# A fused two-block model kernel on one core: router logits from x itself, row lookup in two parts, expert weights loaded slot by slot, biases in four row groups, expert places mixed

## The reference, cut to what matters

```python
x = x + g1[:, None, :] * mix                        # mix = concat(attention, ssm) @ w_out
h = _modulate(_rmsnorm(x, norm2_g[l]), sh2, sc2)    # h = norm(x) * norm2_g * (1 + sc2) + sh2
x = x + g2[:, None, :] * _moe(h, w_router[l], b_router[l], w1[l], b1[l], w2[l], b2[l])
...
logits = (hf @ w_router + b_router).astype(jnp.float32)     # 512 tokens x 32 experts
top_val, top_idx = lax.top_k(logits, TOP_K)                 # TOP_K = 4
gates = jax.nn.softmax(top_val, axis=-1)
...
gu = xb @ w1[e] + b1[e]; gate, up = jnp.split(gu, 2, axis=-1)
glu = gate * jax.nn.sigmoid(SWIGLU_ALPHA * gate)
((up + 1.0) * glu) @ w2[e] + b2[e]                          # per expert, on its own rows only
```

## Time and profile before

| what | value |
| --- | --- |
| median of 3 runs (lowest to highest) | 2327.5 us (2324.67 to 2331.74) |
| the profiled execution | 2333.3 us, span 2332.0 us |
| TensorE clock granted over the span | 0.949 of full speed |
| busy: PE, DVE, ACT, POOL | 91%, 26%, 15%, 2% |
| DMA | 554.64 MB, 238 GB/s over the span |

### The profile page before, as it was taken

The page is one execution under the profiler, slowest core; times in us unless marked ns, Lnnn a source line. Parts: engine busy times, 40 slices in busy tenths (PEclk is TensorE's granted clock), DMA queues, the critical chain, the costliest instruction groups (busy, mean ns, idle before and its releaser), DMA issues.

```text
span 2332.0 us, 35927 instructions
## 1 busy us (share of the span) xinstructions
PE 2121.3 (91%) x15835; PEld 919.6 (39%) x15835; DVE 595.4 (26%) x1120; ACT 353.0 (15%) x607; POOL 46.4 (2%) x54
## 2 busy tenths in 40 slices
PE   5999887699999999999999999736999999899997
PEld 2454444233433334433333333312444444444443
DVE  4983322311111101111110110154044343300002
ACT  2213412000000000000000000003143234200001
POOL 0000000000000000000000000010000000000000
PEclk7999987699999999999999999958999999999999
DMA  7355355696899999999999999660111111122211
GB/s 290 110 198 197 128 225 238 246 376 249 322 414 412 413 405 403 406 404 405 405 407 412 405 406 421 242 251 0 72 54 54 64 63 54 37 78 76 75 42 54
DMA packets 105787, 554.64 MB, mean 238 GB/s; under 512 B 11584, under 2 KB 22976, under 8 KB 56064
## 3 DMA queue, kind: packets, MB, share of 16 engines
q1 hardware_dynamic: 81984, 501.25, 54.1%
q10 hardware_dynamic: 18096, 31.55, 3.7%
q0 software_dynamic: 5552, 19.53, 2.5%
HBM read 525.94 MB, written 26.35 MB: 237 GB/s over the span
## 4 chain that ended last, share of the span: by engine, by line
PE 69%; SPq 12%; DMA 7%; DVE 5%; ACT 5%; issue 2%; ACTq 0%; DVEq 0%
PE psum L690 17%; SPq L325 11%; PE psum L864 10%; PE psum L815 10%; PE psum L698 8%; PE psum L431 6%; DMA arena<-in_w 4%; PE psum L684 3%; PE psum L807 2%; PE psum L873 2%; PE psum L407 1%; DMA ring<-in_mod_slabs 1%; DMA arena<-in_mod_slabs 1%; PE psum L706 1%; PE psum L851 1%
## 5 line engine op out<-in xcount | busy, mean ns | idle before, releaser
L690 PE MATMUL psum<-arena,ring 128*32 128x512 f32 x4288 | 479.9, 602 | 12.6 <-DMA arena<-in_w 12.6
L815 PE MATMUL psum<-h_t,ring 128*128 128x512 f32 x640 | 279.5, 594 | 0.7 <-ACT arena L1170 0.7
L690 PEld LDWEIGHTS psum<-arena,ring 128*32 128x32 f32 x4288 | 134.8, 111 | 357.1 <-issue 323.4
L698 PE MATMUL psum<-arena,h_t 128*32 128x256 f32 x3840 | 213.0, 380 | 9.8 <-DMA arena<-in_w 9.8
L1588 DVE TENSOR_SCALAR h_t<-psum 128x512 f32<-128x512 f32 (+2 forms) x33 | 27.9, 845 | 679.8 <-PE psum L690 679.8
L815 PEld LDWEIGHTS psum<-h_t,ring 128*128 128x128 f32 x640 | 120.6, 190 | 153.4 <-issue 151.9
L698 PEld LDWEIGHTS psum<-arena,h_t 128*32 128x32 f32 x3840 | 122.4, 110 | 92.8 <-DMA arena<-in_w 12.7
L1095 ACT ACTIVATE ring<-psum 128x512 f32<-128x512 f32 (+2 forms) x33 | 23.8, 720 | 740.5 <-PE psum L677 740.5
L690 PE MATMUL psum<-ring 128*32 128x512 f32 x1152 | 129.5, 600 | 5.1 <-DMA ring<-in_w 5.1
L431 PE MATMUL psum<-h_t,ring 128*128 128x512 f32 x256 | 115.0, 605 | 6.8 <-ACT h_t L919 6.8
L864 PE MATMUL psum<-h_t,ring 128*128 128x512 f32 x256 | 115.4, 605 | 4.7 <-DVE arena L1728 4.7
(11 more groups left out here) (390 smaller groups left out, 1738.5 us busy)
## 6 DMA issues: line engine op xcount, KB each, us to landing
arena<-in_w SPq DMA_DIRECT2D x288, 1024.0 KB, 28.1
ring<-in_w SPq DMA_DIRECT2D x96, 1024.0 KB, 29.4
ring<-in_mod_slabs SPq DMA_DIRECT2D x16, 2048.0 KB, 8.8
ring<-in_turn_slabs SPq DMA_DIRECT2D x40, 512.0 KB, 3.3
ring<-in_merge_slabs SPq DMA_DIRECT2D x32, 512.0 KB, 3.3
ring<-in_proj_slabs SPq DMA_DIRECT2D x24, 512.0 KB, 3.6
y_rows<-arena ACTq DMA_DIRECT2D x1, 10752.0 KB, 35.3
y_rows<-work ACTq DMA_DIRECT2D x72, 64.0 KB, 7.6
```

Of the source, the lines that this page charges most:

```text
L690: mm = pe.matmul(psum[32 * j:32 * j + 32, g, :], x_e[:, c * tokens + g * TG:c * tokens + g * TG + TG], slot[s][:, j * S:(j + 1) * S], star ...
L698: mm = pe.matmul(psum[32 * j:32 * j + 32, 6 + g // 2, (g % 2) * 256:(g % 2) * 256 + 256], h_e[:, g * 256 + half * P + 32 * c:g * 256 + hal ...
L815: mm = pe.matmul(psum[:, bank, :], ring[:, s, k, :], h_t[:, k, :], start=(k == 0), stop=(k == KT - 1))
```

## The change

Nothing is added to or taken from the result; the same values are computed by another route.

- The logits are taken from `x_t` itself. The router is scaled once by norm2_g*(1+sc2) (`gain`), and the share of sh2 in the logits is put into `brouter` by nine small matmuls ("router shift"). PE sums the products of four channel tiles each into four column groups (`logit_part`, parts 0 to 3 between slabs 22 and 23), DVE copies the four partial sums, and a matmul with the constant "stack" adds them and turns them to tokens. The root mean square of each token comes out as a column of 128 partitions x 4 (`square_sum`, on squares that DVE has added up on the way), and scales the logits (`row_scale`) and the stored rows. Shift and gain are applied later, in `keep_x`, by eight ACT instructions a pass instead of one.
- The waits of the routing are split (RANKS no longer waits for the "tokens ahead" matmuls), DVE's one-hots are single instructions, and the lookup is made in two parts: rows of the first four passes (`SOON`), then of the other 29. The gates are finished behind the lookup and turned on PE behind the first pass's up chunks.
- SP issues the clearing of `y_rows` and, behind it, 12 of the first 16 weight chunks before the last four slabs of w_out, each when its slot's buffer is free; the last four go out when the last slab has been used.
- b1 is loaded into four row groups of partitions, and the bias matmuls of group g read row group g.
- `PLACES` has another order.

```diff
-PLACES = [0, 1] + [2 + r for r in (15, 0, 16, 17, 1, 18, 2, 19, 3, 20, 4, 21, 5, 22, 6, 23, 7, 24, 8, 25, 9, 26, 10, 27, 11, 28, 12, 13, 14, 29)]
+PLACES = [0, 1, 17, 18, 19, 2, 20, 21, 3, 22, 23, 4, 24, 25, 5, 6, 7, 26, 8, 9, 27, 10, 11, 28, 12, 13, 29, 14, 15, 30, 16, 31]
...
+            sp.wait_ge(sem("arena zeroed"), 1)
+            sp.dma_start(y_rows[PLACE_ROWS:, :].rearrange("(b c) d -> c b d", c=ROWS),
+                         arena[:, 0:D].unsqueeze(1).to_broadcast([P, MAXO, D])).then_inc(sem("y cleared"), 16)
+
+
+            def load_chunk(n, s, e, c):
...
+            sp.wait_ge(sem("y cleared"), 16)
+            sp.wait_ge(sem("mod turned"), 9)
+            load_first(0, 1, 2, 3, 4, 5, 8, 9, 11)
+            sp.wait_ge(sem("head mixed"), 4)
+            load_first(6, 7, 10)
             for n in range(20, 24):
                 load_slab_of(n)
...
+            load_first(12, 13, 14, 15)
...
+            bank = pair_bank("router shift")
+            for k in range(KT):
+                pe.matmul(bank[:, 0:EXPERTS], mods[:, 24 + k:25 + k].to_broadcast([P, P]), router[:, k, :], start=(k == 0), stop=False, skip_group_check=True)
+            pe.matmul(bank[:, 0:EXPERTS], identity, brouter[:, :], start=False, stop=True, skip_group_check=True).then_inc(sem("router shifted"), 1)
...
+            def logit_part(k):
+                rows = slice(32 * (k % 4), 32 * (k % 4) + 32)
+                return pe.matmul(psum[rows, 4, :], router[:, k, :], x_t[:, k, :], start=(k < 4), stop=(k >= 4), skip_group_check=True)
+
+            def square_sum(k, first, last):
+                for t in range(TT):
+                    mm = pe.matmul(psum[:, 1, t:t + 1], h_t[:, k, t * P:(t + 1) * P], ones[:, 0:1], start=(first and t == 0), stop=last, skip_group_check=True)
+                return mm
...
+                if n == 22:
+                    pe.wait_ge(sem("router scaled"), 1)
+                    pe.wait_ge(sem("x mixed"), 4)
+                    for k in range(4):
+                        logit_part(k)
...
+            pe.wait_ge(sem("x mixed"), 7)
+            for k in range(4, 7):
+                logit_part(k)
+            pe.wait_ge(sem("squares added"), 6)
+            square_sum(0, True, False)
             pe.wait_ge(sem("x mixed"), 8)
-            rms_sum(1, h_t)
-            pe.wait_ge(sem("router loaded"), 16)
-            pe.wait_ge(sem("h ready"), 16)
+            logit_part(7).then_inc(sem("routing (PE)"), 1)
+            pe.wait_ge(sem("norm squares"), 16)
+            square_sum(7, False, True).then_inc(sem("norm sum"), 1)
+            pe.wait_ge(sem("routing (DVE)"), LOGIT_PARTS)
...
+                    mm = pe.matmul(psum[32 * g:32 * g + 32, 0, 0:SOON], hot_tok[:, n, :], hot_group[:, n, bass.ds(g, SOON, step=4)], start=(n == 0), stop=(n == TT * TOPK - 1), skip_group_check=True)
...
+                    mm = pe.matmul(psum[32 * g:32 * g + 32, 6, 0:NP - SOON], hot_tok[:, n, :], hot_group[:, n, bass.ds(4 * SOON + g, NP - SOON, step=4)], start=(n == 0), stop=(n == TT * TOPK - 1), skip_group_check=True)
...
-                        pe.matmul(psum[32 * j:32 * j + 32, g, :], which.to_broadcast([EXPERTS, TG]), b1_sb[:, j * S:(j + 1) * S], start=True, stop=False, skip_group_check=True)
+                        pe.matmul(psum[32 * j:32 * j + 32, g, :], which[EXPERTS * g:EXPERTS * g + EXPERTS, :].to_broadcast([EXPERTS, TG]), b1_sb[EXPERTS * g:EXPERTS * g + EXPERTS, j * S:(j + 1) * S], start=True, stop=False, skip_group_check=True)
...
-                act.activation(x_e[:, 0:KT * tokens].rearrange("p (b n) -> p b n", b=2), psum[:, 4:6, 0:4 * tokens], ACT.Copy).then_inc(sem("x_e kept"), 1)
+                for k in range(KT):
+                    act.activation(x_e[:, k * tokens:(k + 1) * tokens], psum[:, 4 + k // 4, (k % 4) * tokens:(k % 4 + 1) * tokens], ACT.Identity,
+                                   bias=mods[:, 24 + k:25 + k], scale=gain[:, k:k + 1]).then_inc(sem("x_e kept"), 1)
...
+            hot_groups(0, SOON).then_inc(sem("routing (DVE)"), 1)
...
```

More of the change, by code:

```diff
@@ L651, in tensor_engine @@
             for t in range(TT):
-                mm = pe.matmul(psum[0:EXPERTS, 2, EXPERTS:EXPERTS + 1], sel[:, t, :], ones[:, 0:1], start=(t == 0), stop=(t == TT - 1), skip_group_check=True)
+                for g in range(4):
+                    mm = pe.matmul(psum[EXPERTS * g:EXPERTS * g + EXPERTS, 2, EXPERTS:EXPERTS + 1], sel[:, t, :], ones[:, 0:1], start=(t == 0), stop=(t == TT - 1), skip_group_check=True)
+            mm.then_inc(sem("routing (PE)"), 1)
             for t in range(TT):
@@ L1056, in scalar_engine @@
             keep_columns(8)
+            act.wait_ge(sem("router shifted"), 1)
+            from_pair("router shift", brouter[:, :])
             head_squares(2)
@@ L1516, in vector_engine @@
-            then(dve.reciprocal(gsum, gsum))
-            for t in range(TT):
-                dve.tensor_scalar(gates[:, t, :], gates[:, t, :], gsum[:, t:t + 1], None, ALU.mult)
-                for k in range(TOPK):
-                    ins = dve.tensor_scalar(onehot[:, t, k, :], const("expert"), idxf[:, t, k:k + 1], None, ALU.is_equal)
-            then(ins)
-            dve.tensor_tensor(sel, onehot[:, :, 0, :], onehot[:, :, 1, :], ALU.add)
-            then(dve.tensor_scalar(gmat[:, 0, :], onehot[:, 0, 0, :], gates[:, 0, 0:1], None, ALU.mult))
@@ L1535, in vector_engine @@
+            then(dve.tensor_reduce(place_col, beats, AX_X, ALU.add))
+            dve.tensor_scalar(chosen_by, const("expert"), place_col, None, ALU.is_equal).then_inc(sem("routing (DVE)"), 1)
             dve.wait_ge(sem("routing (PE)"), PLACES_TURNED)
@@ L1864, in constants @@
     put("partition", p * 1.0)
+    put("row", p % EXPERTS * 1.0)
+    put("stack", (p % EXPERTS == e) * 1.0)
     put("eps", np.full((P, 1), EPS))
```

193 lines of the change are left out of this document (106 added, 87 removed).

## The result

The changed kernel took **2266.1 us** (median of 4 runs, 2264.8 to 2267.4), beside 2326.1 us for the kernel before in the same runs: a ratio of 0.974, 95% interval 0.972 to 0.976. Run again later beside other kernels it took 2263.7 us, again a ratio of 0.974 (0.971 to 0.976). The forecast was 2261 us, the range 2244 to 2287. The profiled execution took 2266.05 us, 67.3 less than that of before.

What follows compares the result with a forecast made beforehand. PE and DMA were taken as both nearly full in the experts, the routing before them as a chain of short steps. Routing -38.3 and experts -28 gave -66: 2267 us profiled, 2261 on the median's scale, range 2244 to 2287.

Steps and rivals of the forecast that it cites:

- Point 1: Ahead of the last "x mixed": router shift 1.9 us and four early logit parts 0.9, together +2.8 us.
- Point 2: From the last "x mixed" to the scaled logits: 4.5 us instead of 35.8, so -31.3.
- Points 3 to 5: Scaled logits to `sel` (-4.0), `sel` to the counts (-2.2), counts to rooms (+2.0).
- point 4: `sel` to the counts on DVE: 3.8 us instead of 6.0, with about 1.3 us of row turning still holding PE.
- Points 6 and 7: Rooms to lookup -2.1 us, as `hot_group` shrinks; lookup to gather 2.8 us as before, the four-column lookup taken at 2.2.
- Point 8: Gather to `turn_x`: 4.6 us instead of 6.1, so -1.5, since PE no longer waits for the gates.
- Point 9: `turn_x` to the first up chunk: 3.4 us instead of 5.4, so -2.0, with a shorter bias beside ACT's `keep_x`.
- Ten us to spare: w_out slab 20 behind clear and twelve chunks: those are through by 328, PE wants the slab at 339.
- Loading early: Loading twelve weight chunks early gains nothing by itself, since all 16 already landed before PE wanted them.
- Bias, 1.0 us a pass: Experts: bias matmuls take 1.0 us a pass whatever its groups, 33 us instead of 77, PE falling to 989 us.
- DMA decides, 26 us idle: Experts: DMA sets the pace with 998.5 us of loading and 26 idle; stage 1034 us, -28.
- The first rival: Bias matmuls in different row groups don't overlap further; PE needs 1033, the new order alone gains 3: 2286, chance 0.13.

Runs made afterwards that it cites:

- The repetition: The changed kernel itself, unaltered, run and profiled again later beside other kernels: 2263.7 us, ratio 0.974.
- experiment 10: The changed kernel with all 33 passes marked and looked up at once again: 2270.0 us, ratio 0.976.
- experiment 11: The changed kernel with first-pass `turn_h` later, router shift moved, and passes 16 to 32 marked before waiting for the first lookup: 2262.5 us.
- experiment 5: The changed kernel with y_rows cleared a second time, ahead of the twelve chunks and slabs 20 to 23: 2291.5 us, ratio 0.985.
- experiment 6: The changed kernel with all sixteen first weight chunks issued behind the last slab's use: 2276.9 us, ratio 0.980.
- experiment 4: The changed kernel with half of chunks 10 and 11 of every expert not loaded, same PE work: 2209.7 us, ratio 0.950.
- experiment 3: The changed kernel with the old order of places and every bias matmul reading row group 0: 2294.6 us, ratio 0.987.
- experiment 1: The changed kernel with every bias matmul reading row group 0: 2273.9 us, ratio 0.978.

## Why the prediction was right, point by point

- **Point 1, +2.8, measured +4.4 in this profile.** The shift took 1.95 and 0.39 us, 2.0 from start to start, and the logit parts 1.06: sized right. Missing was the third output right behind the short matmuls at the lower clock level (granted 0.58 over it), 1.7 us longer. The repetition shows 365.7 and an output at 1.00, so the term is 0 to 6 us by the run.
- **Point 2, -31.3.** Measured 4.9 us from the last "x mixed" to the scaled logits, forecast 4.5. Most of the gain is here, and it came for the stated reason: no wide square, sum, root, product or 64 router matmuls lie behind the last slab.
- **Points 3 to 5.** 4.8, 1.4 and 4.5 us, forecast 4.1, 3.8 and 5.0. The error is in point 4: the turns of rows held PE up for half a us only (it stands in point 3), and the column counts, priced at 1.2 between 0.6 and 2.4, took 0.43, under the lower bound: 32 of them in four column groups cost less than eight alone had at the low clock.
- **Points 6 and 7.** 8.0 and 2.5 us, forecast 7.9 and 2.8. The lookup of four columns took 1.89 us, near the 2.2 taken and far from the 0.3 in proportion to columns. The Trainium skill, TensorEngine Tiling (Array Packing), Instruction Overhead, gives a short matmul the same latency as one with 60 columns; by that rule, the traces nearly agree: 4 columns 1.89, 29 columns 2.15, 33 columns 2.22 for 128.
- **Point 8, 4.6 us, measured 5.5.** Wrong by the mark that runs beside GpSimd's issue (experiments 10 and 11): it was priced as work behind the gather's start, at nothing. The stores were in time.
- **Point 9, 3.4 us, measured 1.6**, in the repetition 2.9. The bias of two groups took 1.09 us in the one and 1.96 in the other, and the first up chunk did not wait for ACT.
- Together 33.3 us where 36.1 were forecast, which with 1.6 lost in the head makes 402.5 and not 403.6: right, with errors of both signs.
- **"Ten us to spare" for slab 20**: a delay of 6 to 10 us at the head of the queue is absorbed (experiment 5), but the slab lands 1 to 3 us before it is wanted. The ledger had clear and chunks through by 328 and the slab lands at 337.6: from 320 to 330 the DMA engines were busy (share 0.99) at 237 GB/s only, so the 2.6 us a chunk did not hold there. **Loading early "is worth nothing by itself"**: wrong, some 12 us (experiment 6); the cover that was named, weights wanted late, is not the only thing the load can hit.
- **Bias, 1.0 us a pass**: 1.09 for two groups, 1.14 for four, 37.7 for all 33 passes where 33 were taken. PE busy in the stage: 986, forecast 989. But busy holds some of the pipeline's waiting; freed of it, PE needs 977 (experiment 4).
- **DMA decides, 26 us idle**: the last loads were issued at 1407.9, and the last chunk landed by about 1434.1 (1435.94 less 1.8 for its matmuls; the last loads took 26.1 at least). 1434.1 - 406.1 - 998.5 - 2 leaves 27.5. PE waited 40.7 us for weights, at the upper end of the 20 to 40 that were forecast. The stage of 1033.5 against 1034, -28.2 against -28, is right in sum and in its parts.
- **The first rival's price was mis-sized.** It put 25 us on bias groups that don't overlap, since PE would need 1033 again and the new order alone would save 3. Measured, that kernel's stage is 1043, so the order alone saves 16 (1058.7 less 1043.1, experiments 3 and 1), and the bias 9.6. The failed step is that PE's 1033 were taken as a floor with all its waits of before on top; the order takes the waits away (PE waits for weights 19.2 us in experiment 3 and 2.6 in experiment 1). Had the rival come true, the time would have been 2274, not 2286.

The forecast of 2261 was 3 to 5 us too low. The profiled execution was forecast at 2267 and took 2266.05; what missed is the 5.8 us by which the profiled run of before lay above its median. The changed kernel's profiled run lay on its own. That 2266.05 comes so close to 2267 is in part luck: the first up chunk was forecast at 403.6 and came at 402.5 here and 400.5 in the repetition, with the head early or late by the run. The stage of the experts repeats within 1 us in these two profiles.

What stays argued: no experiment takes the logits from x alone back to the old route. That it shortens the path by some 31 us is read from the two timelines.

## What to carry to other kernels

When a scale and a shift stand in front of a small product, look whether the raw product can be summed as its inputs come in and the scale and shift be put around it: here 31 us of the critical path went for 3 us of matmuls elsewhere. Where two engines' limits lie within a few per cent (DMA at 1026 us with its idle, PE at 977, or, by an estimate from 46 us more of bias, 1023), price an edit by the limit that is left when the waits have moved, and measure each limit by taking away work of the other. And look at what VectorE does at the moment when GpSimd issues.

## What was not expected of the hardware

- GpSimd's issue of a gather took 1.04 us alone and 1.83 beside a two-input VectorE instruction of 1.28 us, in ten profiles; in the four where nothing of the kind ran beside it (the kernel before, and experiments 6, 10 and 11) 1.04 to 1.07.
- Right behind 18 short matmul instructions (128x32, 2.3 us in most), eight 128x512 ones took 4.0 to 4.6 us in eight of ten profiles, else 2.4. TensorE ran the same instructions ahead of that place in all ten; what decides it stays open.
- The granted clock tells the two cases apart: over the output itself it was 0.50 to 0.59 (the lower level) in all eight profiles with the long output and 1.00 in the other two of the ten, the three with the shift moved, and the kernel before. First the changed kernel, then its repetition:

```profile
282.39:286.48 4.09, 4.09 (x12) 2.31 (x11) 0.00 (x0) 0.20 (x1) 0.00 (x0) 0.58 1.02 419
```

```profile
282.33:284.73 2.40, 2.40 (x12) 1.49 (x11) 0.00 (x0) 0.20 (x1) 0.00 (x0) 1.00 1.02 415
```

Ahead of it TensorE had run 4 us of matmuls with 1 to 32 columns without a gap (from 278.4); where the shift was moved it was 2 us of them, and before the change 2 us as well. In two of the eight, experiments 3 and 10, the shift's own matmuls were long already (3.44 and 2.80 us for 1.95).
- A row store of 512 KB landed 2.6 us after its issue on free DMA engines and 8.1 to 10.6 behind or among weight chunks. The first indirect gather landed 3.8 to 4.2 us after it where its issue took 1.04 to 1.07, 5.3 to 6.3 where VectorE's mark ran beside the issue, and 9.2 among the chunks.
